# An expert's rows gathered as 1 KB quarters and transposed in 32x32 blocks on VectorE; the operands of the list product exchanged

## What is computed

```python
def block_fn(args):
    t_idx, g, e = args                       # rows of one expert, their gates, the expert
    xb = x2d[t_idx]
    hb = jax.nn.silu(xb @ exp_gate[e]) * (xb @ exp_up[e])
    return (hb @ exp_down[e]) * g[:, None]
...
yb = lax.map(block_fn, ...)
routed = jax.ops.segment_sum(yb.reshape(P, -1), buf_t, num_segments=T)
return shared + routed
```

## Time and profile before

| | us |
|---|---|
| median of 3 runs | 1145.57 |
| lowest, highest | 1140.51, 1149.66 |
| span of the profiled execution | 1144.7 |
| PE busy | 1076.1 (94%) |
| DVE busy | 540.9 (47%) |
| ACT busy | 280.5 (25%) |
| POOL busy | 180.2 (16%) |

### The profile page before, as it was taken

How to read it: one execution, slowest core, us unless ns; L and a number is a source line. 1 busy time by engine, 2 the same in 40 slices (tenths; PEclk the granted TensorE clock), 3 DMA queues, 4 the chain that set the end, 5 groups by cost and what they waited for, 6 DMA issues and landing times.

```text
span 1144.7 us, 33418 instructions
## 1 busy us (share of the span) xinstructions
PE 1076.1 (94%) x14942; PEld 814.8 (71%) x14943; DVE 540.9 (47%) x1208; ACT 280.5 (25%) x596; POOL 180.2 (16%) x198
## 2 busy tenths in 40 slices
PE   7999998887899999999999999999999999999990
PEld 6877886765653567677777777777777777777760
DVE  0789969698665778553222222222222222222215
ACT  2156411122337111111111111111111111111114
POOL 2000100000000002122222222122222222222210
PEclk9999999989669999999999999999999999999995
DMA  7222131220425557799999999999999999999734
GB/s 215 74 56 56 50 82 41 49 74 5 162 74 203 172 191 299 282 351 372 368 355 357 362 363 362 359 361 359 366 361 368 364 362 360 363 363 352 221 48 160
DMA packets 87365, 278.79 MB, mean 244 GB/s; under 512 B 22331, under 2 KB 46916, under 8 KB 62381
## 3 DMA queue, kind: packets, MB, share of 16 engines
q1 hardware_dynamic: 71941, 239.29, 57.1%
q0 software_dynamic: 14336, 34.11, 12.6%
q10 hardware_dynamic: 944, 3.24, 0.8%
HBM read 258.80 MB, written 34.52 MB: 256 GB/s over the span
## 4 chain that ended last, share of the span: by engine, by line
PE 67%; DVE 9%; issue 2%; ACT 2%; DMA 1%; SPq 0%; POOLq 0%; DVEq 0%; ACTq 0%
PE ph L2303 30%; PE ph L2331 19%; PE pst L2278 4%; PE ph L1496 2%; PE pz_late L2278 2%; DVE w_exp L163 2%; PE pt L869 1%; PE pst L1392 1%; PE pt L1411 1%; PE ph L1621 1%; PE ph L1478 1%; PE pz_late L1436 1%; PE pz_late L1437 1%; PE pt L1405 1%; PE pt L1414 0%
## 5 line engine op out<-in xcount | busy, mean ns | idle before, releaser
L2303 PE MATMUL ph<-arena,w_exp 128*64 128x96 f32 x8192 | 352.5, 247 | 0.0
L2303 PEld LDWEIGHTS ph<-arena,w_exp 128*64 128x64 f32 x8192 | 340.4, 138 | 4.2 <-issue 3.1
L2331 PE MATMUL ph<-w_exp,arena 128*96 128x512 f32 x512 | 230.5, 593 | 1.2 <-DVE arena L2321 1.2
L2358 POOL DMA_INDIRECT scr_f<-arena,row x64 | 92.3, 1443 | 472.0 <-DMA scr_f<-arena,row 230.1
L2319 DVE TENSOR_TENSOR arena<-arena,ph 128x192 f32<-128x192 f32 x64 | 22.7, 355 | 287.8 <-ACT arena L2312 287.8
L507 PE MATMUL pz<-w_exp 128*128 128x260 f32 x672 | 158.4, 394 | 0.3 <-ACT w_exp L322 0.3
L2331 PEld LDWEIGHTS ph<-w_exp,arena 128*96 128x96 f32 x512 | 80.2, 167 | 103.8 <-issue 102.3
L507 PEld LDWEIGHTS pz<-w_exp 128*128 128x128 f32 x672 | 129.3, 195 | 23.3 <-issue 2.9
L2349 DVE TENSOR_SCALAR arena<-ph,weight 96x512 f32<-96x512 f32 x64 | 47.8, 746 | 174.2 <-PE ph L2331 174.1
L2312 ACT ACTIVATE arena<-ph 128x192 f32<-128x192 f32 x64 | 21.1, 330 | 416.0 <-PE ph L2303 416.0
L163 DVE SCALAR_TENSOR_TENSOR w_exp<-arena,w_exp 128x512 f32<-128x512 f32 x120 | 90.0, 750 | 3.8
(11 more groups left out here) (359 smaller groups left out, 1076.4 us busy)
## 6 DMA issues: line engine op xcount, KB each, us to landing
w_exp<-in_exp_up_dram SPq DMA_DIRECT2D x64, 1024.0 KB, 17.3
w_exp<-in_exp_down_dram SPq DMA_DIRECT2D x64, 1024.0 KB, 16.5
w_exp<-in_exp_gate_dram SPq DMA_DIRECT2D x64, 1024.0 KB, 13.7
w_exp<-in_w_in_dram SPq DMA_DIRECT2D x22, 512.0 KB, 3.9
w_exp<-in_x_prompt_dram SPq DMA_DIRECT2D x8, 512.0 KB, 5.2
w_exp<-in_w_out_dram SPq DMA_DIRECT2D x2, 2048.0 KB, 11.5
scr_x<-arena SPq DMA_DIRECT2D x4, 512.0 KB
scr_f<-arena ACTq DMA_DIRECT2D x4, 512.0 KB, 3.6
```

Of the source, the lines that this page charges most:

```text
L2303: last = nc.tensor.matmul(pgu[64 * half:64 * half + 64, s % 2, (2 * part + j) * CAP:(2 * part + j + 1) * CAP], w[job.slot][:, k, f0:P * ha ...
L2331: last = nc.tensor.matmul(pyl[0:CAP, c, :], hid[:, s % 2, j, :], m.expert_down[job.slot][:, j, c * 512:(c + 1) * 512], start=(j == 0), sto ...
L2358: nc.gpsimd.indirect_dma_start(m.scr_f, bass.IndirectOffsetOnAxis(ap=row[:, job.l:job.l + 1], axis=0), y_list[:, s % 2, :], None, bounds_c ...
```

## The change

- The list product has its operands exchanged: a window of `table` (32 columns, of which 6 count) is stationary and `member` moves with 96 columns. The result has the 6 entries on partitions and the slots in columns.
- `read_list` turns it back with a DVE transpose in 32x32 blocks, so a slot lies on partition t of block r (slot 32r + t, 3 blocks). Row numbers are made for each of the four quarters of a row, on four groups of 32 partitions (`piece_row`), and row number and weight are also copied to one slot per partition, for the scatter and the weighing.
- `gather` issues three indirect DMAs of 128 partitions, one per block. Each slot is fetched as four pieces of 1 KB, quarter c on partition group c.
- One DVE transpose in 32x32 blocks (`turn_pieces`) writes `x_list_t` in the layout as before. The 8 PE transposes and the 2 ACT copies of an expert are gone.
- On DVE the order of an iteration is now: read list q+4, transpose q+2, build `member` q+5, `gate_mul` q+1, weigh q. Before the loop, expert 0 is transposed ahead of the last residual and expert 1 behind it.
- The counting of full lists moves from before the first residual into expert 0's iteration.
- Some small tiles move into the space of `x_area`. The fallback keeps its way of working.

```diff
 def make_list(nc, m, pe, job, pl):
...
     for i in range(NT):
-        last = nc.tensor.matmul(pl[0:CAP, s % 2, 0:6], m.member[:, s % 2, i, :],
-                                m.table[:, bass.ds(q, 1), i, :].rearrange("p o c -> p (o c)"),
+        at = (q * NT + i) * 6
+        last = nc.tensor.matmul(pl[0:32, s % 2, 0:CAP], m.table_rows[:, at:at + 32], m.member[:, s % 2, i, :],
                                 start=(i == 0), stop=(i == NT - 1))
...
 def read_list(nc, m, dve, ch, job, pl):
...
-    nc.vector.tensor_copy(entry[:, s, :], pl[0:CAP, s % 2, 0:6]).then_inc(m.entry_ready, 1)
+    nc.vector.transpose(entry[:].rearrange("t r j -> t (r j)"), pl[0:32, job.s % 2, 0:CAP]).then_inc(m.entry_ready, 1)
     dve.wait_ge(m.entry_ready, q + 1)
-
-    nc.vector.tensor_scalar(spare[:, s:s + 1], entry[:, s, 2:3], m.minus_spare[0:CAP, :], m.spare_row[0:CAP, :], ALU.mult, ALU.add)
-    nc.vector.scalar_tensor_tensor(token[:, s:s + 1], entry[:, s, 0:1], float(P), entry[:, s, 1:2],
-                                   ALU.mult, ALU.add).then_inc(m.rows_ready, 1)
-    dve.wait_ge(m.rows_ready, 2 * q + 1)
-    nc.vector.tensor_tensor(row[:, s:s + 1], spare[:, s:s + 1], token[:, s:s + 1], ALU.add).then_inc(m.rows_ready, 1)
-    nc.vector.tensor_reduce(weight[:, s:s + 1], entry[:, s, 3:6], AX, ALU.add).then_inc(m.weight_ready, 1)
+    ch.link(nc.vector.scalar_tensor_tensor(found[:, :, 0], entry[:, :, 0], float(P), entry[:, :, 1], ALU.mult, ALU.add))
+    ch.link(nc.vector.scalar_tensor_tensor(found[:, :, 0], entry[:, :, 2], -float(TT), found[:, :, 0], ALU.mult, ALU.add))
+    for quad in range(QUADS):
+        last = nc.vector.tensor_scalar(m.piece_row[32 * quad:32 * (quad + 1), s, :], found[:, :, 0],
+                                       float(QUADS), float(QUADS * TT + quad), ALU.mult, ALU.add)
+    last.then_inc(m.pieces_ready, 1)
+    ch.link(nc.vector.tensor_reduce(found[:, :, 1], entry[:, :, 3:6], AX, ALU.add))
+    for r in range(RUNS):
+        last = nc.vector.tensor_copy(m.row_weight[32 * r:32 * (r + 1), s, :], found[:, r, :])
+    ch.link(last)
+    nc.vector.tensor_scalar(m.row[:, s:s + 1], m.row_weight[0:CAP, s, 0:1], float(TT), None, ALU.add).then_inc(m.weight_ready, 1)
 
 
 def gather(nc, m, pool, job):
...
-    pool.wait_ge(m.rows_ready, 2 * q + 2)
+    pool.wait_ge(m.pieces_ready, q + 1)
     if job.has_before(NB):
-        pool.wait_ge(m.x_turned, 2 * (q - NB + 1))
+        pool.wait_ge(m.x_ready, q - NB + 1)
     pool.sem_inc(m.waits_over)
-    nc.gpsimd.indirect_dma_start(m.x_list[:, s, :], None, m.scr_x1,
-                                 bass.IndirectOffsetOnAxis(ap=m.row[:, job.l:job.l + 1], axis=0),
-                                 bounds_check=TT - 1, oob_is_err=False).then_inc(m.gathered[s], 16)
+    for r in range(RUNS):
+        nc.gpsimd.indirect_dma_start(m.x_pieces[:, s, r, :], None, m.scr_x1.rearrange("t (q c) -> (t q) c", q=QUADS),
+                                     bass.IndirectOffsetOnAxis(ap=m.piece_row[:, job.l, r:r + 1], axis=0),
+                                     bounds_check=QUADS * TT - 1, oob_is_err=False).then_inc(m.gathered[s], 16)
...
-    def turn_list(pe, job):
...
-    def copy_turned(act, job):
...
+    def turn_pieces(dve, job):
         q, s = job.q, job.s
+        dve.wait_ge(gathered[s], 16 * RUNS * (job.turn + 1))
+        if job.has_before(2):
+            dve.wait_ge(gu_done, q - 1)
+        nc.vector.transpose(x_list_t[:, s % 2].rearrange("p k (r t) -> p r k t", r=RUNS),
+                            m.x_pieces[:, s].rearrange("p r (c k) -> p r k c", k=KD)).then_inc(x_ready, 1)
...
             if q + AHEAD < E:
-                read_list(nc, m, dve, Job(q + AHEAD), pl)
+                read_list(nc, m, dve, ch, Job(q + AHEAD), pl)
+            if q + 2 < E:
+                turn_pieces(dve, Job(q + 2))
+            if q + AHEAD + 1 < E:
+                build_member(nc, m, dve, Job(q + AHEAD + 1))
             if q + 2 < E:
                 gate_mul(dve, Job(q + 1))
-            if q + AHEAD + 1 < E:
-                build_member(nc, m, dve, Job(q + AHEAD + 1))
```

More of the change, by code:

```diff
@@ L52 @@
 SLOTS = 6
+QUADS = 4
+QW = D // QUADS
+RUNS = CAP // 32
 STEPS = 2 * NB
@@ L868, in make_list, with read_list @@
     for i in range(NT):
-        last = nc.tensor.matmul(pl[0:CAP, s % 2, 0:6], m.member[:, s % 2, i, :],
-                                m.table[:, bass.ds(q, 1), i, :].rearrange("p o c -> p (o c)"),
+        at = (q * NT + i) * 6
+        last = nc.tensor.matmul(pl[0:32, s % 2, 0:CAP], m.table_rows[:, at:at + 32], m.member[:, s % 2, i, :],
                                 start=(i == 0), stop=(i == NT - 1))
     last.then_inc(m.list_done, 1)
-def read_list(nc, m, dve, job, pl):
+def read_list(nc, m, dve, ch, job, pl):
     q, s = job.q, job.l
-    entry, spare, token, row, weight = m.entry, m.spare, m.token, m.row, m.weight
+    entry, found = m.entry, m.found
     dve.wait_ge(m.list_done, q + 1)
@@ L1835, in store_f @@
                     act.dma_start(m.scr_f[t0:t0 + n, :], x1[0:n, i, :]).then_inc(m.f_stored[i], 16)
-                for i in range(TM - 1):
+                for i in range(TM):
                     store_f(i)
-                work.copy_turned(act, Job(0))
-                store_f(TM - 1)
                 act.wait_ge(f_done, NT)
@@ L2114, in _ @@
                     build_member(nc, m, dve, Job(q))
-                nc.vector.memset(cnt[:, 1:4, :], 0.0)
-                ch.link(nc.vector.tensor_copy(cnt[:, 0, :], ppos[:, NT, :]))
-                for b in range(1, m.MAX_JOBS):
-                    ch.link(nc.vector.tensor_scalar(cnt[:, 2, :], cnt[:, 0, :], float(b * CAP), None, ALU.is_gt))
-                    ch.link(nc.vector.tensor_tensor(cnt[:, 1, :], cnt[:, 1, :], cnt[:, 2, :], ALU.add))
-                ch.link(nc.vector.tensor_tensor_scan(cnt[:, 2, :], m.ones[:, 0:E], cnt[:, 1, :], 0.0, ALU.mult, ALU.add))
+                nc.vector.tensor_copy(cnt[:, 0, :], ppos[:, NT, :])
                 def residual(i):
@@ L2340, in weigh_act @@
             act.wait_ge(added[s % 2], 16 * job.pair)
-        nc.scalar.activation(y_list[:, s % 2, 0:512], pyl[0:CAP, 0, :], ACT.Copy, scale=weight[:, job.l:job.l + 1]).then_inc(y_act, 1)
+        nc.scalar.activation(y_list[:, s % 2, 0:512], pyl[0:CAP, 0, :], ACT.Copy, scale=row_weight[0:CAP, job.l, 1:2]).then_inc(y_act, 1)
     def weigh_dve(dve, job):
@@ L2348, in weigh_dve @@
             dve.wait_ge(added[s % 2], 16 * job.pair)
-        nc.vector.tensor_scalar(y_list[:, s % 2, 512:1024], pyl[0:CAP, 1, :], weight[:, job.l:job.l + 1], None, ALU.mult).then_inc(y_dve, 1)
+        nc.vector.tensor_scalar(y_list[:, s % 2, 512:1024], pyl[0:CAP, 1, :], row_weight[0:CAP, job.l, 1:2], None, ALU.mult).then_inc(y_dve, 1)
     def add_rows(pool, job):
@@ L2445, in vector @@
         ch = Chain(dve, m.vector_step, m.vector_count)
+        cnt = m.cnt
         def count_jobs(part):
             if part == 0:
+                ch.link(nc.vector.memset(cnt[:, 1:4, :], 0.0))
+                for b in range(1, m.MAX_JOBS):
+                    ch.link(nc.vector.tensor_scalar(cnt[:, 2, :], cnt[:, 0, :], float(b * CAP), None, ALU.is_gt))
+                    ch.link(nc.vector.tensor_tensor(cnt[:, 1, :], cnt[:, 1, :], cnt[:, 2, :], ALU.add))
+                ch.link(nc.vector.tensor_tensor_scan(cnt[:, 2, :], m.ones[:, 0:E], cnt[:, 1, :], 0.0, ALU.mult, ALU.add))
                 upto = m.cnt[:, 2, :].unsqueeze(1).broadcast_to([P, m.EXTRA, E])
```

70 lines of the change are left out of this document (26 added, 44 removed).

## The result

The changed kernel takes 1117.22 us (1113.35 to 1118.35) against 1147.16 us (1140.51 to 1149.66) of the kernel before in the same session: ratio 0.9733, 95% interval 0.9695 to 0.9772. The forecast of 1146 us, no change, was wrong; the time lies inside the range of 1110 to 1170.

The account below looks back on a forecast made before the run. PE at 10.11 us per expert, with an equally long scatter chain taking over. Scatter 0 plus 1.2, six periods at 9.4, 49 at 10.45 put scatter 55 4.9 later; tail minus 3.9: plus 1.0, forecast 1146 us, range 1110 to 1170.

Parts of the forecast that it names:

- The order of bounds: Expert loop: PE and DMA engines both full; scatters, a second chain as long as PE's, would rule once PE is quicker.
- below 90%: Sign that the scatter chain rules: PE share below 90%, with waits at the down product or at weighing.
- PE's relief: PE per expert: transposes minus 0.97 us, list product minus 0.07, so the period falls from 10.11 to 9.07 us.
- The DMA engines: An expert's traffic needs about 10.30 us; smaller gather pieces and skipped slots add 0.1 to 0.3, taken as 0.1.
- The scatter chain: Scatters queue behind three gathers of 128 slots; period taken as 10.45 us, bounds 10.30 to 10.44 and 10.4 + 3.
- the first six periods: Scatter periods at the loop's start, while the load queue is short: 9.4 us each, 56.4 in all.
- rival A: Slower: quartered gathers hold the scatter up; scatter period 10.6 to 11.1 us, 1154 to 1178 us; chance 0.33.
- Rival B: Faster: loads are the floor at 10.3 to 10.4 us, scatter latency near 8.5; 1110 to 1115 us; chance 0.17.
- VectorE: Block transpose 1.04 us (bounds 0.65 to twice 1.04), `read_list` plus 1.0; work per expert about 4.7 us, from 2.65.
- The last sentence of the prediction: Forecast is wrong if gathers arrive so late that PE waits for VectorE's transpose and not for the scatter.
- The start: Start of the loop unmoved, bounds 3 us either way; counting in expert 0's turn makes scatter 0 1.2 us later.
- The tail: After scatter 55 PE sets the end again, with four transposed lists less: minus 3.9 us.

Follow-up runs that it names:

- after_noscatter: The changed kernel without its scatter-adds and the waits on them; 1094.73 us, ratio 0.9567.
- two_turns: The kernel before with two of an expert's eight PE transposes and the old 96-partition gather, turned rows wrong; 1134.65 us, ratio 0.9917.
- wide: two_turns with the gather of whole 4 KB rows over 128 partitions, the upper 32 out of bounds; 1106.27 us, ratio 0.9677.
- quarters96: two_turns with each gather split into four of 1 KB quarters, still on 96 partitions; 1152.08 us, ratio 1.0066.
- before_wide: The kernel before with the whole-row gather over 128 partitions, all eight PE transposes kept; 1144.95 us, ratio 1.0008.
- before_4k: The kernel before with each 1 MB weight load issued as two of 4 KB per partition; 1140.76 us, ratio 0.9975.
- after_4k: The changed kernel with each 1 MB weight load issued as two of 4 KB per partition; 1099.75 us, ratio 0.9603.

## Why the prediction was wrong, point by point

**The order of bounds: right.** That two resources are full, that the scatter chain would take over, and how that shows (waits of weighing for scatters, a PE share below its former one) came as written; "below 90%" did not, PE is at 93%.

**PE's relief: right in kind, too large.** The transposes went, 0.97 us. But down gave back 0.17 and the list product 0.04 (0.32 for 0.28) instead of gaining 0.07: 10.11 - 9.36 = 0.75 us an expert, not 1.04 (after_noscatter).

**The DMA engines: the step that failed.** I took 10.30 us per expert as what the traffic needs and added 0.1 for smaller pieces. The 10.30 was read correctly, and two_turns confirms it (10.26), but it was no property of the bytes. It held the price of a 96-partition gather running beside 128-partition loads: with the gather over 128 the same loads took 0.282 us a packet for 0.308, and the period fell to 9.81 (`wide`). The part "the quarters" of the diff I costed by number and size of pieces, and I never asked what their new spread over partitions does to the transfers beside them. The 0.1 that I added did not come either: q0's packets took 12.6% of 1144.7 = 144 us of the 16 engines before and 12.7% of 1116.1 = 142 after. Its reason, that skipped slots carry no data, holds for q0's bytes but not for the memory (`wide`); the bytes that are read stayed the same, since 124 skipped pieces of 1 KB are as much as 31 of 4 KB.

**The scatter chain: the term mis-sized.** Term by term, against the sum: scatter 0 came 5.2 us after the forecast 490.5; the first six periods took 62.3 us for 56.4 (scatter 6 at 557.97), plus 5.9, as a scatter already landed after a median 9.3 us at 500 to 600 us; the next 49 took 474.9 for 512.1, 9.69 us each, minus 37.2; the rest 57.9 for 61.6, minus 3.7. Together minus 29.8, the miss of the span (1116.1 for 1145.7, minus 29.6). The period is the term that failed, 9.69 us where 10.45 was taken, and the two ahead of it hid 11.1 of its 37.2 us. Of the bounds that I gave it the lower was 10.30; none lay below today's value, since I had excluded a gain without a row that did so. That three gathers of 24 slots per engine stand ahead of a scatter cost nothing that shows: q0 has 16384 packets for 14336, 32 more per list, though a list has 288 more slots. after_noscatter has 9216, that is 144 for each of 64 gathers, and so 112 for a scatter; before, the two together had 14336/64 = 224, 112 each if the scatter's number is the same. 96 packets of data and 16 more for each issue would give both numbers, so a gather's data came in as many packets as before. The rule of the Trainium skill cited with rival A (DMA: Bandwidth & Descriptors, the descriptor table: a packet preferably up to 4096 B, so four quarters make one) agrees with that count.

**Rival B** named the right condition, a landing that stays near 8.5 us, and so came nearest with its 1110 to 1115; it missed by 2 us, and had only 0.17. Its floor of 10.3 to 10.4 us was wrong: the loads did not run out of slots or time (12.2 us to land). The rule of the Trainium skill weighed in the prediction (DMA: Bandwidth & Descriptors, "Where 436 GB/s comes from", about 358 GB/s) is not borne out here either: the five windows of 100 us from 500 on moved 377 to 388 GB/s. **Rival A** did not occur; the nearest thing to it is quarters96, 1152 us at 10.32 us per scatter, still short of A's 10.6.

**VectorE.** The block transpose took 1.57 us, half more than the 1.04 taken and inside the bounds; `read_list` came to about 2.5 us for 0.8 before, plus 1.7 where 1.0 was forecast. In the stretch of the earlier trace rows DVE has 352.97 us for some 61 experts, 5.8 each where 4.7 was forecast. The last sentence of the prediction came true in small: DVE's transpose waits 33 times for its gather (25.2 us), `member` stands behind it, and for `member` PE waits 3.5 of its 10.7 idle us.

**The start: wrong by 5 us.** I had scatter 0 later by 1.2, it came 6.4 later. VectorE's timeline at expert 0 shows the counting ahead of the weighing; its first and its twelfth instruction, then L2444, which stood before the weighing in the kernel before too:

```profile
487.93 0.22 DVE L2438 MEMSET cnt<- 128x192 f32 x1
...
490.63 0.29 DVE L2442 TENSOR_TENSOR_SCAN cnt<-ones,cnt 128x64 f32<-128x64 f32 x1
490.96 3.02 DVE L2444 TENSOR_TENSOR arena<-cnt,job_index 128x2752 f32<-128x2752 f32 x1
494.01 0.75 DVE L2338 TENSOR_SCALAR arena<-ph,row_weight 96x512 f32<-96x512 f32 x1
```

The 12 small ones cost 3.0 us there (487.93 to 490.96), the most that was forecast; the rest is a later gate/up 0, which I had taken as unmoved. On PE, its line:

```profile
472.80 8.15 PE L2292 MATMUL ph<-arena,w_exp 128*64 128x96 f32 x128 [5.22 <-issue]
```

It waits 5.22 us for the first transpose on VectorE (471.16 to 472.70), which stands behind residuals and list work, and then takes 8.15 us instead of 5.51. It starts only 1.2 us later than before (471.60); the other 2.6 are the clock. The granted clock was 0.66 from 472.8 to 481.0 us, between the lower level of 1.2 GHz and the higher of 2.4, and it had already fallen to 0.50 at 471.8 us, while PE stood idle. So gate/up 1 began at 481.20 for 477.36: 3.8 us, above my bound of 3.

**The tail**: from scatter 55 to 63 it took 57.9 us for 65.5 before, minus 7.6 where minus 3.9 was forecast. What the other 3.7 are was not taken apart.

**A reading.** The DMA engines are at nine tenths from the 18th slice on, 486 us, not from 515; nothing in the sum rests on it.

## What to carry to other kernels

An indirect transfer on fewer partitions than the bulk loads beside it can slow those loads, here by some 9% per packet where the DMA engines were pressed (0.308 us in two_turns for 0.282 in `wide`), and not measurably in the time where TensorE set the pace (before_wide); when two streams share the DMA engines, compare their spread over partitions before their bytes. A pace read from a trace (10.30 us per expert) is the price of that mixture of transfers, not a floor of the chip; a change that alters the form of one of them opens that number on both sides. And where two chains are equally long, a change to one alone will show nothing: two_turns, before_wide and before_4k each moved the time by less than 1%, and together such parts are worth 2.7% (changed), 3.2% (`wide`) and 4.0% (after_4k).

## What was unexpected of the hardware

- 4 KB rows over 128 partitions instead of 96, 32 of them skipped: 1106.27 against 1134.65 us.
- Slots out of bounds are not free: 32 more per list raised HBM reads by 8.39 MB in the gathers and HBM writes by 8.39 MB in the scatters, the full size of the rows, while q0's own bytes hardly rose (34.12 and 34.16 MB for 34.11 and 34.14).
- Loads in packets of half the size landed scatters 0.7 us sooner (8.3 for 9.0) though the engines moved less (375 to 380 GB/s in the windows from 500 us on, for 377 to 388).
- TensorE can pause in a stream of matmuls for 0.16 to 0.42 us at a time, at most experts, and the profile names nothing that it waits for; the kernel with these pauses took 52 us more. Whether an edit of a few us in the start or the chip set them off is open.
- A 128 x 768 block transpose of 32-bit elements on VectorE took 1.57 us.
